# Down projection of a hybrid residual block: twelve pairs of k-tiles as seven block products each, their weight sums on GpSimd

## What is computed

```
n1  = rmsnorm(x);  q|k|v|o|i|f|x_r|g_r = n1 @ w_in
x   = x + concat(mLSTM heads, RG-LRU blocks) @ w_out          # the mixer
n2  = rmsnorm(x);  gate, up = split(n2 @ w_up)                # 2048 -> 2 x 5632
gate = causal_dwconv(gate)                                    # width 3
x   = x + (silu(gate) * up) @ w_down                          # 5632 -> 2048, the stage called down
y   = rmsnorm(x)
```

## Time and profile before

| | us |
|---|---|
| median of three runs (1128.97 to 1131.03) | 1129.88 |
| the profiled execution | 1129.11 |
| its span, first to last instruction | 1127.3 |
| TensorE busy in the span | 1116.9 |
| VectorE, ScalarE, GpSimd busy | 738.9, 581.5, 48.1 |
| the stage down, first matmul to last | 880.5 to about 1120 |

### The profile page before, as it was taken

One profiled execution on the slowest core, in us unless ns is written; L12 is line 12 of the kernel. 1 busy time (PEld: TensorE's weight loads), 2 busy tenths in 40 slices (PEclk: granted clock), 3 DMA queues, 4 the chain that ended last, 5 costly groups with the idle time before them and its releaser, 6 DMA issues.

```text
span 1127.3 us, 18124 instructions
## 1 busy us (share of the span) xinstructions
PE 1116.9 (99%) x6022; PEld 963.0 (85%) x6022; DVE 738.9 (66%) x992; ACT 581.5 (52%) x792; POOL 48.1 (4%) x44
## 2 busy tenths in 40 slices
PE   8999999999999999999999999999999999999997
PEld 8888888888888888888888888888888888888886
DVE  6677585675776676676666666666766755557554
ACT  7656475564756554444444435444444545455454
POOL 0100000001000000000000000000000000001000
PEclk9999999999999999999999999999999999999999
DMA  8766647566565566566656655665665665655653
GB/s 261 229 169 193 181 138 231 149 193 191 188 205 174 179 197 192 169 189 206 189 161 211 197 187 168 208 193 175 184 207 189 192 195 190 195 190 196 194 191 112
DMA packets 166553, 213.04 MB, mean 189 GB/s; under 512 B 6988, under 2 KB 149584, under 8 KB 166400
## 3 DMA queue, kind: packets, MB, share of 16 engines
q1 hardware_dynamic: 165504, 210.40, 60.5%
q0 software_dynamic: 448, 1.78, 0.5%
q10 hardware_dynamic: 576, 0.53, 0.1%
HBM read 210.58 MB, written 2.10 MB: 189 GB/s over the span
## 4 chain that ended last, share of the span: by engine, by line
PE 98%; ACT 1%; DMA 1%; SPq 0%; DVE 0%; issue 0%; DVEq 0%; ACTq 0%
PE ps L1146 42%; PE ps L1287 29%; PE ps L1148 21%; PE ps L1143 2%; PE ps L1144 1%; DMA xres<-x_dram 1%; PE ps L1257 1%; PE ps L1129 0%; ACT xn L368 0%; PE ps L1108 0%; PE ps L1231 0%; ACT w L368 0%; SPq L290 0%; PE ps L1176 0%; PE ps L1233 0%; PE ps L1252 0%
## 5 line engine op out<-in xcount | busy, mean ns | idle before, releaser
L1146 PE MATMUL ps<-xT,w 128*128 128x512 f32 x2048 | 715.5, 395 | 0.0
L649 DVE TENSOR_TENSOR w<-raw,w 128x1024 fp32r<-128x1024 f32 x388 | 476.0, 1239 | 330.5 <-ACT w L368 329.7
L368 ACT ACTIVATE w<-raw 128x1024 fp32r<-128x1024 f32 (+2 forms) x397 | 410.4, 1046 | 403.6 <-PE ps L1148 241.6
L1148 PE MATMUL ps<-xT,w 128*128 128x256 f32 x2048 | 569.1, 278 | 0.0
L1146 PEld LDWEIGHTS ps<-xT,w 128*128 128x128 f32 x2048 | 384.1, 188 | 89.3 <-issue 0.2
L1148 PEld LDWEIGHTS ps<-xT,w 128*128 128x128 f32 x2048 | 385.1, 188 | 0.3
L1287 PE MATMUL ps<-w,aT 128*128 128x512 f32 x1440 | 327.3, 389 | 0.0
L1287 PEld LDWEIGHTS ps<-w,aT 128*128 128x128 f32 x1440 | 270.0, 188 | 56.0
L368 ACT ACTIVATE fs<-fc 128x512 f32<-128x512 f32 x22 | 13.9, 632 | 101.1 <-DVE fc L1031 101.1
L1092 POOL TENSOR_TENSOR fs<-fs,rB 128x512 f32<-128x512 f32 x22 | 28.5, 1297 | 568.6 <-ACT fs L368 568.6
L655 DVE TENSOR_TENSOR aT<-act,aT 128x256 fp32r<-128x256 f32 x88 | 38.9, 442 | 0.0
(11 more groups left out here) (152 smaller groups left out, 391.4 us busy)
## 6 DMA issues: line engine op xcount, KB each, us to landing
raw<-w_up_dram SPq DMA_DIRECT2D x176, 512.0 KB, 4.6
raw<-w_in_dram SPq DMA_DIRECT2D x92, 512.0 KB, 3.9
raw<-w_down_dram SPq DMA_DIRECT2D x88, 512.0 KB, 4.6
raw<-w_out_dram SPq DMA_DIRECT2D x32, 512.0 KB, 4.4
raw<-w_in_dram SPq DMA_DIRECT2D x8, 256.0 KB, 6.7
xres<-x_dram SPq DMA_DIRECT2D x3, 512.0 KB, 7.1
y_dram<-xn SPq DMA_DIRECT2D x3, 384.0 KB, 3.1
gfin<-gfin_dram POOLq DMA_DIRECT2D x1, 1024.0 KB, 5.3
```

Of the source, the lines that this page charges most:

```text
L368: return sc.activation(out_, in_, fn, **kw)
L649: v.tensor_tensor(w[:, s, :, 1, :], raw[:, s, :].rearrange("p (c n) -> p c n", c=CH), w[:, s, :, 0, :], ALU.subtract).then_inc(lo_ready, 1)
L1146: mm(full, w[:, s, c, 0, cut], xT[:, kt, :, :].rearrange("p a n -> p (a n)"), start=kt == 0, stop=False)
L1148: ins = mm(rest, w[:, s, c, 1, cut], xT[:, kt, 0, :], start=False, stop=kt == KT - 1)
```

## The change

In each half, 6 of the 22 pairs are taken out of the ring and computed by a form of Strassen's algorithm. With rows in two blocks, k in two tiles and columns in two blocks of 512, a pair is a 2x2 by 2x2 block product; it takes seven block products of three matmuls each (21) in place of eight (24). A half is now body 0, pair 0, body 1, pair 1, ..., body 5, pair 5, body 6, last body: 8 bodies of four units and 6 pairs.

- Seven weights per pair: B11, B21, B22 and four sums T1 to T4. GpSimd forms the sums (`weight_sums`: one subtraction of 128x1024 and two of 128x512, each waiting for the one before).
- Activation sums S1 to S4 are made once by VectorE in the stage before (`row_sums`, four operations of 128x128 in every third iteration) and serve both halves.
- ScalarE and VectorE split the seven weights and eight activation blocks: three operations of 128x512 and three of 128x1024 on each engine and pair (`pair_hi`, `pair_lo`). Their targets `s_w` and `s_act` and the raw weights `s_raw` exist once and lie over `xT` and `xn`.
- The products that several outputs share accumulate in four more banks, those of the other half. At the end of a half ScalarE copies one bank and VectorE adds them up in six operations (`pairs_out`), interleaved with the splitting of the last units.
- Half 1 begins on TensorE only after `xd0`, the last of those six, and its first pair after `out1_0`, which empties half 0's ordinary banks. GpSimd's sums for half 1 wait for `xd0` too.

Core of the diff:

```diff
+PERIODS = 6
+PERIOD = RING + 2
-DOWN_BODIES = FT // RING
+DOWN_BODIES = (FT - 2 * PERIODS) // RING
...
+            def load_pair(half, b):
+                if half or not isinstance(b, int):
+                    sp.wait_ge(s_lo_ready, (b + half * PERIODS) * S_PARTS)
+                for k in range(2):
+                    sp.dma_start(s_raw[:, 2 * k:2 * k + 2, :]...).then_inc(s_landed, 16)
...
+            load_body(G_DOWN, w_down, 0, 0)
+            after(sp, A2, "std1")
+            load_pair(0, 0)
...
+            def pair_hi(half, b, buffers_free):
+                p = b + half * PERIODS
+                act_e.wait_ge(s_landed, p * S_LOADS + S_LOADS)
+                act_e.wait_ge(*buffers_free)
+                act_fn(s_w[:, B11, 0, :], s_raw[:, 0, :]).then_inc(s_hi_ready, 1)
+                act_fn(s_w[:, B21:B22 + 1, 0, :], s_raw[:, 2:4, :]).then_inc(s_hi_ready, 1)
+                act_fn(s_act[:, 0, 0, :], act[...]).then_inc(s_hi_ready, 1)
+                act_fn(s_act[:, 1, 0, :], s_sum[...]).then_inc(s_hi_ready, 1)
+                act_e.wait_ge(t_summed, p * T_SUMS + 1)
+                act_fn(s_w[:, T1:T3 + 1, 0, :], t_sum[:, 0:2, :]).then_inc(s_hi_ready, 1)
+                act_e.wait_ge(t_summed, p * T_SUMS + T_SUMS)
+                act_fn(s_w[:, T2:T4 + 1, 0, :], t_sum[:, 2:4, :]).then_inc(s_hi_ready, 1)
...
+            def down():                                   # VectorE
+                for half in range(2):
+                    pair_lo(half, 0)
+                    if half == 1:
+                        for r in range(ROWS):
+                            add_residual(V4, ED, G_DOWN, DOWN_BODIES, r, 0)
+                    split_body(act, g0 + 1, PERIOD, tiles + RING)
+                    with dve.Fori(1, PERIODS) as b:
+                        pair_lo(half, b)
+                        split_body(act, b + (g0 + 1), ...)
+                    parts = pairs_out(half)               # xa u xu z xz xd
+                    for s in range(RING):
+                        split_units(g0 + DOWN_BODIES - 1, [s])
+                        split_tiles(act, FT - RING, ..., [s])
+                        next(parts)
+                    for s in range(RING):
+                        if half == 0:
+                            split_units(g0 + DOWN_BODIES, [s])
+                            split_tiles(act, 0, ..., [s])
+                        if s < 2:
+                            next(parts)
...
+            def weight_sums(half, b):                     # GpSimd
+                pool.wait_ge(s_landed, p * S_LOADS + S_LOADS)
+                if half or not isinstance(b, int):
+                    pool.wait_ge(s_lo_ready, p * S_PARTS)
+                sub(t_sum[:, 0:2, :], s_raw[:, 1:4:2, :], s_raw[:, 0:2, :], ALU.subtract).then_inc(t_summed, 1)
+                pool.wait_ge(t_summed, p * T_SUMS + 1)
+                sub(t_sum[:, 2, :], s_raw[:, 3, :], t_sum[:, 0, :], ALU.subtract).then_inc(t_summed, 1)
+                pool.wait_ge(t_summed, p * T_SUMS + 2)
+                sub(t_sum[:, 3, :], s_raw[:, 2, :], t_sum[:, 2, :], ALU.subtract).then_inc(t_summed, 1)
+            for half in range(2):
+                if half == 1:
+                    after(pool, V4, "xd0")
+                weight_sums(half, 0)
+                with pool.Fori(1, PERIODS) as b:
+                    weight_sums(half, b)
...
+            def pair(half, b, opens=False, closes=False): # TensorE
+                for n, m, bank, parts in ((A11, B11, own + BANK_A, 4), (A12, B21, bank0, 4), (S4, B22, bank0 + 1, 4),
+                                          (S1, T1, own + BANK_D, 5), (S3, T3, own + BANK_E, 5),
+                                          (S2, T2, own + BANK_C, 6), (A22, T4, bank0 + 2, 6)):
+                    pe.wait_ge(s_lo_ready, p * S_PARTS + parts)
+                    for a_part, w_part in ((0, 0), (0, 1), (1, 0)):
+                        ins = mm(ps[:, bank, :], s_act[:, n // 4, a_part, cut], s_w[:, m, w_part, :], ...)
+            def down():                                   # TensorE
+                for half in range(2):
+                    if half == 1:
+                        after(pe, V4, "xd0")
+                    body(where, 0, opens=True)
+                    ...
+                    if half == 1:
+                        after(pe, V4, "out1_0")
+                    pair(half, 0, opens=True)
+                    with pe.Fori(1, PERIODS - 1) as b:
+                        body(where, b)
+                        pair(half, b)
+                    ...
```

More of the change, by code:

```diff
@@ L628, in _ @@
             after(act_e, V3, "act", UP_ITERS - 1)
[L629 removed]
+            down()
             for r in range(ROWS):
@@ L1048, in _ @@
                 gate_post(j * 2 + (n_up + 2), j + 1)
+            with dve.Fori(0, PERIODS) as b:
+                for n in range(3):
+                    up(b * 3 + n)
+                row_sums(b * 3 + 2, b)
+            with dve.Fori(3 * PERIODS, UP_ITERS - 1) as j:
+                up(j)
             for s in range(RING):
@@ new lines, in body, with last_body, out_products @@
+            def body(where, b, **ends):
+                for s in range(RING):
+                    for r in range(ROWS):
+                        half_unit(*where, b, s, r, **ends)
+            def last_body(where, b, late=None):
+                for r in range(ROWS):
+                    for s in range(RING):
+                        half_unit(*where, b, s, r, closes=True)
+                        if r == 1 and s == 1 and late:
+                            late()
+            def out_products(early, late):
@@ L1270, in contraction @@
                 for half in range(2):
-                    bank0 = 4 * (1 - half)
+                    where = G_OUT, OUT_BODIES, 0, half, E2
                     if half == 1:
[L1273 to L1291, removed]
-                                did(ins, E, "row1_1")
-                        if last and r == 0:
-                            did(ins, E, f"row0_{half}")
-                        if r == ROWS - 1:
-                            ins.then_inc(unit_used, 1)
@@ L1298, in body @@
-                    def body(b, **ends):
-                        for s in range(RING):
-                            for r in range(ROWS):
-                                half_unit(b, s, r, **ends)
-                    body(0, opens=True)
-                    if half == 1 and early:
-                        body(1)
-                        early()
-                    with pe.Fori(2 if half == 1 and early else 1, bodies - 1) as b:
-                        body(b)
-                    for r in range(ROWS):
-                        for s in range(RING):
-                            half_unit(bodies - 1, s, r, closes=True)
-                            if half == 1 and r == 1 and s == 1 and late:
-                                late()
+                        pe.wait_ge(group_free, G_OUT + FREE_AT_START)
```

209 lines of the change are left out of this document (173 added, 36 removed).

## The result

| | before | after |
|---|---|---|
| median, us | 1129.62 (1128.97 to 1131.03) | 1134.99 (1133.92 to 1135.96) |
| ratio | | 1.0045, 95% interval 1.0034 to 1.0056 |
| the profiled execution, its span | 1129.11, 1127.3 | 1133.92, 1131.9 |
| granted clock | 0.999 | 0.995 |

The account below looks back on a forecast made before the run. The prediction took TensorE to bound the kernel, down being one unbroken run of matmuls. Its terms, -8.16 + 2.3 + 1.5 + 2.7 + 4.3 + 0.25 = +2.9 us, gave 1132.8 us against 1129.88, range 1124.3 to 1145.

Parts of the forecast that it names:

- Who bounds down, and the 8.16 us: In down only TensorE ends last; removing 36 matmuls of 0.2267 us there saves 8.16 us.
- The price of GpSimd's sums: In down, each pair's sums close VectorE's two-input SBUF work for 2.28 + 2 x 1.17 = 4.62 us.
- Who has asked goes next: At the SBUF port shared by VectorE and GpSimd, the engine that has already asked gets the next turn.
- The steady excess: Half 0's five later periods of body and pair: 0.3 us each over TensorE's need, 1.5 us in all.
- the upper bound of 0.5: Most excess per period, in us, from GpSimd's durations as reported (5.0 us) in place of what it held.
- the port sets the pace: Rival in down's periods: turn-taking makes a period 16.4 us, +0.8, costing 8 us in place of 1.5; 1140; chance 0.20.
- Border, first pair, start: TensorE stalls: 2.7 us between the halves, 4.3 us before half 1's first pair, 2.3 us at down's start.
- A gap inside a body: Sign in TensorE's timeline: gaps in the middle of bodies would show the prediction wrong; no size given.
- Half 1 without excess: In half 1 the stall between the halves gives VectorE a lead that pays for the periods' excess.
- The clock: Rival: after the 4.3 us stall TensorE runs one pair at 1.2 GHz, 4.8 us more, 1137.6; chance 0.10.

Follow-up runs that it names:

- the last profile of the experiments: Changed kernel with VectorE's order altered (sums on GpSimd) and each pair's loads issued after GpSimd's third sum, 3.4 us earlier: 1131.08 us, ratio 1.0006.
- the second profile: The changed kernel run once more, unaltered: 1135.59 us, profiled at 1135.20.
- the order experiment: Changed kernel with xz0 and xd0 ahead of half 1's splits and out0_0, out1_0 inside its first pair_lo, sums on GpSimd: 1131.44 us, ratio 1.0012.

## Why the prediction was right, and where it wasn't

**Who bounds down, and the 8.16 us.** Right; 8.1 us appeared where nothing stood in the way.

**The price of GpSimd's sums.** Right: held times of 2.28 and 1.17 us, taken from two stretched operations and one, gave 7.6 us for the turn-taking of the steady period, and 7.5 were measured. (The second 2.28 was worked back from the first: by the rows, 1020.11 to 1022.32, it is 2.2, and so it is in the kernel before with GpSimd's sums.) Cutting the sums short or moving them to VectorE removes start, excess and most of the first pair's wait. The Trainium skill's rule ("SBUF — State Buffer", section "Who interferes with whom") holds in its first part, exclusion. Of its second, that whoever issues first gets the port, the last profile of the experiments shows a limit: an operation that asked at 949.10 was passed over by the seven that VectorE began after it.

**"Who has asked goes next."** This step failed as a rule. It held in rows 6, at down's start and at the border. It didn't with the early loads, and once in the changed kernel itself:

```profile
1021.76 4.25 POOL L1250 TENSOR_TENSOR t_sum<-s_raw 128x1024 f32<-128x1024 f32 x1 [11.65 <-DMA s_raw<-w_down_dram]
```

It ends at 1026.01, so it got the port near 1023.7, when VectorE's run of splits was over (its last began at 1023.34). The forecast was hardly touched, since either order adds up to nearly the same.

**The steady excess.** Forecast 0.3 a period, 1.5 us; 1.5 in one profile, 2.9 in the other. Single periods cost 0.19 to 0.61 us in the first and 0.41 to 0.86 in the second, whose mean of 0.59 is above the upper bound of 0.5. So the exact hit in the first profile is partly luck. The forecast took the size from a sum of busy times and left out that the sums begin only when the load has landed, which adds idle time of the port (0.3 us in the period shown, 0.4 in the same period of the second profile). The rival "the port sets the pace" was thus half right: in half 0 it does, at 0.3 to 0.6 us a period instead of 0.8, and in half 1 it doesn't reach TensorE.

**Border, first pair, start.** 2.7, 4.3 and 2.3 forecast, 2.6, 3.9 and 2.2 measured. Reading VectorE's list off the diff with durations from the rows was enough. The start's total is partly luck, for its places were wrong: 1.0, 1.1 and 0.2 were forecast before units 0 and 1 and pair 0, and measured were 0.8 before unit 2 and 1.4 before the pair, in the second profile 2.2 before the pair. The load had landed later than assumed (GpSimd asked at 880.29 and not at 878.0). A gap inside a body, named as a sign of being wrong, stands only there, where the forecast itself had put one.

**Half 1 without excess.** Right, and borne out by the order experiment, which took the lead away and got 3.1 us of excess.

**The clock.** Named as a rival at 4.8 us with a chance of 0.10; it came on top of the forecast and cost 1.7. The size was wrong, since the low stretch covered less than a pair, and the chance too low: the fall before this pair came in both profiles. It should have been a term, not a case.

**The difference of 2.5 us** between +2.9 and +5.4 is thus the clock (1.8) and the larger periods of half 0 (1.4), less 0.4 before the first pair; the rest are small terms. These are the terms of the second profile, in which down grew by the 5.4 us that the medians show; the first profile's sum is +3.9. Why half 0 costs more in one execution than in another stays open.

## What to carry to other kernels

Before work goes to GpSimd, add the held time of its SBUF-reading operations to VectorE's two-input work of the same period and compare with the bound engine's period; here 11.1 + 4.6 stood against 15.64, and VectorE doing the sums itself needed 11.1 + 2.3. Where a stage changes hands, write out the in-order list between the last free slot and the wait, and put what the bound engine waits for first. A gap can carry the next stage's slack: remove it and the excess shows up behind it.

## What the hardware showed beside that

- GpSimd can be kept from the port for 5.3 us (949.10 to about 954.4) while VectorE issues two-input operations back to back, and was for 2 us at 1021.76; at 1003.17 and in rows 6 it got its turn after one. What decides it stays open.
- TensorE at 1.2 GHz: behind gaps of 3.6 us it fell in all three profiles that have one. Behind gaps of 2.5 us at the border it fell in two of six (the changed kernel, and with earlier loads, where body 0 took 12.78 us); behind 2.0 us before half 1's first pair in one of two, and in none of three behind 2.0 us before half 0's first pair (the changed kernel again, and both with earlier loads). Each fall cost 1.5 to 1.8 us of work. The Trainium skill ("TensorE: Matmul & The Clock Gate", Part 1) says that an idle TensorE is throttled to half rate; these profiles agree where it fell, and show that the slow stretch can begin after TensorE has started again (full clock from 1003.14 to 1004.00, 0.50 from 1004.5 on).
- The contraction with w_out began at 301.2 to 303.6 us in the thirteen profiles, though the code before that point computes the same. The spread is nearly half of this change's effect. The first 128x512 matmuls of the kernel begin at 22.4 to 23.8 us, so 1.4 of the 2.4 us are there by then; where the rest arises stays open.
